# Four head-pair bodies of the rwkv branch in one stage, with the front of the next one in the tail of each

## The reference, cut to what matters

```python
def step(s, inp):                       # rwkv7_scan, one token
    r_t, w_t, k_t, v_t, kk_t, a_t = inp
    sa = jnp.einsum('bhvk,bhk->bhv', s, -kk_t)
    s = (s * w_t[:, :, None, :] + sa[..., None] * (kk_t * a_t)[:, :, None, :]
         + v_t[..., None] * k_t[:, :, None, :])
    return s, jnp.einsum('bhvk,bhk->bhv', s, r_t)
y = (rwkv7_scan(r, heads(w_f), k, v, kk, a, False)
     + rwkv7_scan(r, heads(w_b), k, v, kk, a, True))
```

## Time and profile before

| | us |
|---|---|
| median of 3 runs | 1971.18 (1970.96 to 1972.32) |
| the profiled execution, own time | 1972.61 |
| span of its records | 1970.8 |
| PE busy | 1836.0 (93%) |
| DVE busy | 1036.5 (53%) |
| ACT busy | 618.9 (31%) |
| mean granted PE clock | 0.971 of full |
| the four bodies, first sums to the last L2612 | 1329.4 to 1507.6 |

### The profile page before, as it was taken

How to read it: one execution, slowest core, us unless ns; L and a number is a source line. 1 busy time by engine, 2 the same in 40 slices (tenths; PEclk the granted TensorE clock), 3 DMA queues, 4 the chain that set the end, 5 groups by cost and what they waited for, 6 DMA issues and landing times. The chain is left out here.

```text
span 1970.8 us, 38928 instructions
## 1 busy us (share of the span) xinstructions
PE 1836.0 (93%) x16056; PEld 1323.0 (67%) x16056; DVE 1036.5 (53%) x2067; ACT 618.9 (31%) x1338; POOL 81.7 (4%) x59
## 2 busy tenths in 40 slices
PE   5999999999999999998888799979889899999997
PEld 2566666666666666544666687767776687888886
DVE  3567676767676776211135468774555792320101
ACT  2335344544444453202024243233332440100000
POOL 1000000001010110000000000010000000000000
PEclk7999999999999999998999899989999899999999
DMA  9131313111111112031311433231102223443434
GB/s 355 68 99 43 109 44 109 54 66 44 34 34 33 35 44 77 0 135 68 114 63 43 158 135 115 78 115 56 48 34 77 85 108 111 167 154 145 170 150 150
DMA packets 52237, 183.63 MB, mean 93 GB/s; under 512 B 5856, under 2 KB 9312, under 8 KB 51808
## 3 DMA queue, kind: packets, MB, share of 16 engines
q1 hardware_dynamic: 52064, 181.18, 25.5%
HBM read 179.06 MB, written 2.10 MB: 92 GB/s over the span
## 5 line engine op out<-in xcount | busy, mean ns | idle before, releaser
L878 PE MATMUL banks<-u,w_ring 128*128 128x512 f32 x768 | 367.6, 604 | 5.1 <-DVE u L711 5.1
L379 PE MATMUL banks<-u,w_ring 128*128 128x256 f32 x1056 | 250.9, 389 | 8.4 <-PEq L188 8.4
L379 PEld LDWEIGHTS banks<-u,w_ring 128*128 128x128 f32 x1056 | 199.3, 195 | 42.3 <-issue 17.5
L878 PEld LDWEIGHTS banks<-u,w_ring 128*128 128x128 f32 x768 | 138.3, 192 | 115.0 <-issue 103.5
L403 PE MATMUL banks<-u,w_ring 128*128 128x256 f32 x640 | 138.4, 379 | 0.5 <-PEq L188 0.5
L403 PEld LDWEIGHTS banks<-u,w_ring 128*128 128x128 f32 x640 | 121.5, 190 | 17.3 <-issue 0.8
L910 DVE SCALAR_TENSOR_TENSOR acc<-raw,hc,acc 128x512 f32<-128x512 f32 x128 | 107.8, 842 | 4.5
L3476 PE MATMUL banks<-gated,w_ring 128*128 128x512 f32 (+1 forms) x288 | 96.8, 498 | 1.8 <-PEq L188 1.8
L3476 PEld LDWEIGHTS banks<-gated,w_ring 128*128 128x128 f32 x288 | 54.6, 190 | 44.1 <-issue 40.8
L3476 PE MATMUL banks<-ffn,w_ring 128*128 128x256 f32 x352 | 77.9, 385 | 3.0 <-PEq L188 3.0
L3476 PEld LDWEIGHTS banks<-ffn,w_ring 128*128 128x128 f32 x352 | 68.0, 193 | 12.9 <-issue 3.3
(11 more groups left out here) (530 smaller groups left out, 3081.2 us busy)
## 6 DMA issues: line engine op xcount, KB each, us to landing
w_ring<-in_w SPq DMA_DIRECT2D x289, 512.0 KB, 5.5
gated<-in_ada SPq DMA_DIRECT2D x32, 512.0 KB, 4.6
h<-in_h SPq DMA_DIRECT2D x2, 2048.0 KB, 10.7
hold<-h SPq DMA_DIRECT2D x1, 1024.0 KB, 5.2
h<-hold SPq DMA_DIRECT2D x1, 1024.0 KB, 9.4
out<-u SPq DMA_DIRECT2D x8, 128.0 KB, 1.9
const_base<-in_const SPq DMA_DIRECT2D x1, 896.0 KB, 13.1
const_part<-in_const SPq DMA_DIRECT2D x1, 640.0 KB, 4.5
```

What stands on the lines that cost most here:

```text
L379: mm = self.nc.tensor.matmul(place, self.st.chunk(g % 2, slot)[:, P * k:P * k + P], self.src(k), start=(k == 0), stop=(k == KT - 1))
L878: mm = nc.tensor.matmul(self.places[m % len(self.places)][:, :], (st.slot(m) if g is None else st.chunk(g % 2, m))[:, P * k:P * k + P], u[ ...
```

## The change

- The four bodies become one stage. Semaphores count on through the bodies (`due_in(i)`), and the ring is run by `in_stage`: SP loads the weights of body g + 1 once the three tiles of body g - 1 are summed. `BesideGroups` takes the place of `Beside`; its tiles all go through bank 5 (the very last one through bank 7).
- The sums of body i + 1 stand behind wu of body i, in banks 6 and 7, where 4 products stood. ACT's exponentials follow its wu copies and stand ahead of its m_t copies; DVE does the keys of d = 0 ahead of `own_part`, those of d = 1 behind it, and the two reads (one product each) behind q_t. PE does the scores of d = 0 ahead of the last read of the states, and grams 0, scores 1 and grams 1 behind it. `e_in` gets a second buffer.
- The y0 matmuls are in two halves (`start_values`), one ahead of step 1, one between the steps.
- In a level PE does border 0, border 1, then both turns into bank 4; ACT copies all 512 columns at once. Each update waits for that copy. In level 1 the order is border 0, turns, products, border 1.
- The products move into the levels by a table. A pair is (products ahead of the updates, products behind them); the first number is what stands ahead of level 1. In body 0, 8 products stay in the front, and in the last body 4 stand behind wu.

```diff
+    FILL = ((0, ((0, 0), (0, 2), (1, 2), (1, 2), (4, 4))), (1, ((4, 3), (0, 2), (1, 2), (1, 2), (4, 4))),
+            (1, ((4, 3), (0, 2), (1, 2), (1, 2), (2, 2))))
-                extra.products(pe, 4)
+            if last:
+                ahead(per_body * KT * RW - extra.part)
+            else:
+                sums(pe, i + 1)
...
+            start_values(0)
+            pe.wait_ge(s["m_ready"], due("m_ready", 4))
+            if not last:
+                pe.wait_ge(s["exps"], due_in(i + 1)("exps", 2))
+            step(1)
+            start_values(1).then_inc(s["y0_sum"], 1)
+            step(2)
+            pe.wait_ge(s["q_ready"], due("q_ready", 2))
+            of_state(1)
+            of_state(2)
+            if not last:
+                scores(pe, i + 1, 0)
+            pe.wait_ge(s["s_ready"], due("s_ready", 6))
+            of_state(3).then_inc(s["qs_done"], 1)
+            if not last:
+                grams(pe, i + 1, 0)
+                scores(pe, i + 1, 1)
+                grams(pe, i + 1, 1)
...
+            for lv in range(1, levels):
+                border(lv, 0)
+                if lv == 1:
+                    turn(0)
+                    ahead(after[0][0])
+                    pe.wait_ge(s["masked"], due("masked", 1))
+                    border(1, 1)
+                else:
+                    border(lv, 1)
+                    turn(lv - 1)
+                if lv == 2 or lv == 3:
+                    keys_turned(lv - 2)
+                if lv == 4:
+                    own_values()
+                if lv > 1:
+                    ahead(after[lv - 1][0])
                 for d in range(2):
+                    update(lv, d)
+                ahead(after[lv - 1][1])
...
+            for lv in range(levels - 1):
+                act.wait_ge(s["t_turned"], due("t_turned", lv + 1))
+                if lv >= 1:
+                    act.wait_ge(s["bc_done"], due("bc_done", 2 * lv))
+                link(nc.scalar.activation(inv_t[:, :, :, :].rearrange("p d n e -> p (d n e)"), bank[4][:, :], ACT.Copy), s["t_out"])
...
+            if not last:
+                keys(dve, link, i + 1, 0)
+            dve.wait_ge(s["n_sum"], due("n_sum", 2))
+            for d in range(2):
+                own_part(d, 0, s["s_ready"])
...
+            if not last:
+                keys(dve, link, i + 1, 1)
+            dve.wait_ge(s["ms_done"], due("ms_done", 2))
```

More of the change, by code:

```diff
@@ new lines, in rwkv_heads @@
+    per_body = 3
+    counts = {"sums": 2, "exps": 2, "keys": 8, "k_turned": 2, "turned_out": 2, "lt_sum": 2, "lt_out": 2, "grams_done": 2, "masked": 2,
+              "x_sum": 1, "x_in": 2, "a_done": 2 * (levels - 1), "p_ready": 2 * (levels - 1), "t_turned": levels - 1,
+              "t_out": levels - 1, "bc_done": 2 * (levels - 1), "t_ready": 2 * levels, "wu_sum": 2, "wu_act": 2, "wu_dve": 2,
+              "mq_sum": 2, "m_ready": 4, "q_ready": 2, "n_sum": 2, "s_ready": 6, "ms_done": 4, "y0_sum": 1, "y0_out": 2, "qs_done": 1,
+              "y_done": 1}
@@ L2526, in _ @@
-                for d in range(2):
-                    act.wait_ge(s["wu_sum"], d + 1)
-                    link(nc.scalar.activation(wu[half(0), d].rearrange("p n e -> p (n e)"), bank[2 * d][half(0), :], ACT.Copy), s["wu_act"])
-                extra.copy_tile(act, link)
-                act.wait_ge(s["mq_sum"], 2)
-                for c in range(1, 3):
-                    for hh in range(2):
-                        out = m_t[half(hh), :, c - 1, half(hh)]
-                        have = bank[4 + c % 2][half(hh), :].rearrange("p (d t e) -> p d t e", d=2, t=ST)[:, :, c // 2, 0:64]
-                        link(nc.scalar.activation(out, have, ACT.Copy), s["m_ready"])
@@ L2615, in rwkv_heads @@
-    st.begin(3)
-    for i in range(RW):
-        body(i)
-        st.turn(3)
-    st.at += 3 * RW
+                    dve.wait_ge(s["bc_done"], due("bc_done", 2 * (lv - 1) + d + 1))
+                    dve.wait_ge(s["t_turned"], due("t_turned", lv))
+                    link(nc.vector.tensor_tensor(by_head(inv[:, d]), by_head(inv[:, d]), parts(pair(2 * d, 0, P)), ALU.subtract),
+                         s["t_ready"])
+                if lv == 1:
+                    masked(0)
+            for d in range(2):
+                dve.wait_ge(s["wu_sum"], due("wu_sum", d + 1))
+                link(nc.vector.tensor_copy(wu[half(1), d].rearrange("p n e -> p (n e)"), bank[2 * d + 1][half(1), :]), s["wu_dve"])
@@ new lines, in vector_body @@
+            if not last:
+                keys(dve, link, i + 1, 0)
+            dve.wait_ge(s["n_sum"], due("n_sum", 2))
+            for d in range(2):
+                own_part(d, 0, s["s_ready"])
+            for k in range(1, 3):
+                for d in range(2):
+                    own_part(d, k)
+            if not last:
+                keys(dve, link, i + 1, 1)
+            dve.wait_ge(s["ms_done"], due("ms_done", 2))
+            for d in range(2):
+                next_state(d, 1)
@@ new lines, in vector_body @@
+            dve.wait_ge(s["m_ready"], due("m_ready", 4))
+            for d in range(2):
+                have = pair(4, SEQ * d, SEQ * d + SEQ).rearrange("p f (t x) -> p f t x", t=ST)[:, :, :, 64:P]
+                link(nc.vector.tensor_tensor(split(q_t[:, d, :]), have, split(kr[:, d, 1, :]), ALU.add), s["q_ready"])
+            if not last:
+                reads(dve, link, i + 1)
+            dve.wait_ge(s["ms_done"], due("ms_done", 4))
+            for d in range(2):
+                next_state(d, 2)
@@ new lines, in vector_body, with _ @@
+            dve.wait_ge(s["qs_done"], due("qs_done", 1))
+            dve.wait_ge(s["y0_out"], due("y0_out", 2))
+            link(nc.vector.tensor_tensor(y_all[:, :, mine].rearrange("p t (h e) -> p h t e", h=2), parts(pair(4, 0, P)),
+                                         y0[:, :, :].rearrange("p t (h e) -> p h t e", h=2), ALU.add), s["y_done"])
+        @block.tensor
+        def _(pe):
+            sums(pe, 0)
+            extra.products(pe, 5)
+            scores(pe, 0, 0)
+            grams(pe, 0, 0)
+            extra.products(pe, 3)
+            scores(pe, 0, 1)
+            grams(pe, 0, 1)
+            for i in range(RW):
+                tensor_body(pe, i)
@@ new lines, in _ @@
+        @block.scalar
+        def _(act):
+            link = Chain(act, s["act_own"])
+            exponents(act, link, 0, 0)
+            exponents(act, link, 0, 1)
+            for i in range(RW):
+                scalar_body(act, link, i)
+        @block.vector
+        def _(dve):
+            link = Chain(dve, s["dve_own"])
+            keys(dve, link, 0, 0)
+            keys(dve, link, 0, 1)
+            reads(dve, link, 0)
+            for i in range(RW):
+                vector_body(dve, link, i)
@@ L2622, in rwkv_output @@
+    st.passed(RW, per_body)
 def rwkv_output(nc, st, bank, C, y, v_all, g_t, bonus, ln_rows, sq, st16, out, u, ff, lf, kf, lb, om):
```

490 lines of the change are left out of this document (237 added, 253 removed).

## The result

| | before | after |
|---|---|---|
| median of 5 runs, us | 1972.12 (1970.96 to 1972.55) | 1958.86 (1955.60 to 1963.35) |
| ratio, 95% interval | | 0.9934 (0.9922 to 0.9947) |
| profiled execution, own time | 1972.61 | 1963.0 |
| its span | 1970.8 | 1961.2 |
| in front of the stage's first sums | 1329.4 | 1330.5 |

The time lies in the range predicted with 8 in 10 (1948 to 1962), 4.4 us above the predicted 1954.5 and outside the forecast's own range, 1951.5 to 1957. The ratio is 13.0 us of 1972.12 (10.5 to 15.4), and 16.8 were forecast. So the working of the stage held in the main, and the missing part lies outside it.

The account below looks back on a forecast made before the run. PE, busy 93% of the span, and its waits were taken as the bound. Three borders and the last body's level 5 save 17.4 us, the end 3.0, body 0 loses 3.65: 16.8 saved, 1954.5 us, 8-in-10 range 1948 to 1962.

Parts of the forecast that it names:

- the forecast's own range: Whole kernel: 1951.5 to 1957 us around the predicted 1954.5, given chance 0.55.
- The period of a steady body: Stage: tail with front 15.1 plus levels 5.6, 3.95, 4.15, 4.55, 5.6 make 38.95 us, against 44.21.
- Body 0: First body: late grams and products added to its levels lose 3.65 us, moved there from the tail.
- The last body: Four products less in level 5 save 1.65 us more; 12.2 us from the last wu to the end.
- The equal 16.8: Whole saving forecast: 17.4 + 3.0 - 3.65 = 16.8 us.
- The single copy: Levels: one ACT copy makes a level's chain 0.7 us longer, hidden by what stands between turns and updates.
- The price of a change of tiles: PE: changing from 128x128 to 64x64 tiles costs 0.21 us, entered as 0.2.
- The clock: Steady bodies counted at full clock, since products fill the place whose idle preceded half clock in body 1.
- the dip stays: Rival: PE idle before level 2 keeps half clock there, 1.2 us in each steady body, 1958 us; chance 0.2.
- Edits put at nothing: Weight loads, one bank for all tiles, stage ends and longer semaphore counts: no cost; semaphores -0.5 to +0.5 in all.

Follow-up runs that it names:

- once more: The kernel after, run and profiled again with no edit: median 1959.88 us, ratio to before 0.9924, stage 164.5 us.
- tail: Kernel after, last body: level 5's four products move away, the stage's last four go behind step 2: 1958.88 us, ratio 0.9929.
- keys: Kernel after with DVE doing next_state(1) and q_t ahead of the keys of d = 1, next_state(2) ahead of the reads: 1958.72 us, ratio 0.9919.
- two copies: Kernel after with the single ACT copy of both turns split in two, both behind both turns: 1961.92 us.
- light after: Kernel after with one product of eight for each tile in the stage, projection incomplete: 1945.17 us.
- order: Kernel after with the turn of d = 0 put back between the two borders in levels 2 to 5: 1961.85 us.
- fill0: Kernel after with body 0's products as in the steady bodies, four in its level 1: 1959.09 us, ratio 0.9928.
- serial: Kernel after with each body's front put back behind the tail of the one before, product table changed with it: 1973.29 us, ratio 1.0000.
- light before: Kernel before with one product of eight for each tile in the stage, projection incomplete: 1950.52 us.

## Why the prediction was right, and what it missed

- *The period of a steady body*: 38.95 predicted, 38.85 measured twice in the first profile, 38.95 and 38.91 once more. The terms are within 0.16 each in levels 2 to 5, and 0.2 too short for the tail. PE waits 1.57 us in a period, 1.5 were laid out.
- *Body 0*: 3.65 lost predicted. It took 33.1 to wu, 30.3 before, 2.8 lost in the first profile; 34.6 and 4.3 once more. It varies with its half clock. Before had 7.3 us of it there. The tail and keys kernels, with 7.4 and 7.6, took 34.1, which is 3.8 lost.
- *The last body*: its level 5 is 1.6 shorter, as predicted (1.65), but its period is 38.77, not 37.3, as 3.4 us at half clock in its front cost 1.5. From the last wu to the end of DVE's add 12.2, as predicted.
- *The equal 16.8 is in part luck*: in the first profile the three periods gave 16.2 (17.4 predicted), body 0 lost 2.8 (3.65), and from the last wu to the next stage's first matmul it gave 3.4 (3.0). These misses cancel. Once more the parts were 16.0, 4.3 and 3.4, which is 15.1.
- *The single copy is hidden in levels 3 to 5, and a level's chain is 3.3 us without products*: shown by two copies and by light after.
- *The price of a change of tiles* was 0.2 in the sum; by order it is 0.3 for the way there and back.
- *The clock*: 1.00 in two of the three later bodies, against the Trainium skill, "TensorE: Matmul & The Clock Gate" (A second HAM failure mode: psum-queue depth-cycling), that the prediction cites; 3.4 us of half clock in the third. That fall comes at 1453.60, behind a wait of 0.43 us and at the one of 0.74, and the two other bodies have these waits as well. So what decides is not shown. The rival "the dip stays" came true once instead of three times. The median, 1958.86, is nearest to that rival's 1958, but not for its reason: its stage would have been 3.6 us longer than forecast.
- *Edits put at nothing*: behind its first sums, PE waits in the stage of the kernel after for no load of weights and for no copy of a tile; the longest waits there are 0.75 us, and all are for DVE. In fill0 a tile's copy did hold it, for 1.16.
- *The overlap is the gain*: serial, 13.8 of 16.8 us in the stage: 11.5 at full clock in both, the rest the dips of the clock that come back without the overlap.
- *The step that was missing*: nothing was put down for the work behind the stage. It lasted 461.8 us in both profiles of before and 463.8 to 468.1 in the ten others without filled idles. In all fourteen profiles this length follows the half clock in it: a straight line through them is 450.2 plus 0.51 us for each us at half clock, no profile off by more than 0.9. The one stage can't be its only cause, since light before, with four stages and the old loads, has 466.0. A stall of the same length, 2.96 us ahead of the stage behind swiglu, is followed by 0.76 over 7 us in one kernel and 0.58 in another. That it depends on when in time the stall comes fits this, and stays argued: no run moved the stage's end alone. It took back 3.2 us in the second profile of after and 6.1 in the first, of 15.1 and 16.8 gained in the stage.

## What to carry to other kernels

Where bodies in a row are bound by PE plus short chains, put the front of the next one into the tail of the last before tuning inside: here the stage gained 13.8 of its 16.8 us by that, 11.5 of them without any help from the clock. Filling the levels with other work was worth at most 1.9 us of 5.4 in a body, and part of it may be the clock. Add up PE's order with one price for each group and one for each change of tile shape, and find the engine whose unbroken chain sets the waits that remain. Do not take the stages behind as fixed: a gain can be partly given back there to the clock. Unread matmuls in an idle of 3 us in front of dense work are then worth a try: they brought the kernel before to 0.9971 (0.9960 to 0.9982). And compare two orders only with the half clock of each beside it.

## What the runs showed of the hardware

- A change between 64x64 and 128x128 tiles and back costs 0.30 to 0.32 us of PE's time where PE is the bound.
- PE idle for 2.96 us in front of dense matmuls is followed by half clock within the next 7 us (0.58 or 0.76 granted); with the idle filled to 0.41 it was 1.00, in both kernels tried.
- The same kernel's times spread by 8 us in five runs (1955.6 to 1963.35). Over fourteen profiles, the part behind the stage is longer by 0.51 us for each us at half clock in it.
- Half clock can follow waits much shorter than 2.96 us: before, it came behind a stretch with PE busy 0.84 of 2.50 us; level 2 then lasts 4.94 us, and 3.95 in light before, where it runs at full clock.
